# RWKV stage of a one-core decoder step: eight gate steps of each pair placed elsewhere, the h chunk loaded in halves, constants and states loaded after the first h

## The chip, the core and the metric

The program runs on one core of a Trainium2 chip. The metric is the device time of one execution in microseconds, lower is better. A number is the median of several executions; one further execution is profiled, and all rows below are from that one.

## What is computed

One layer of a hybrid decoder over 1024 prompt rows and 8 x 8 sample rows (1088 columns in the transposed layout that the kernel uses). Only the RWKV branch, and the sigmoid gates that the merge needs later, are touched by the change:

```python
mixed = cur + (prev - cur) * p['rwkv_mu']
r, wd, k, v, ad, gd = _split(mixed, RWKV_SPLIT)
w_log = -jax.nn.softplus(-(p['rwkv_w0'] + jnp.tanh(wd) @ p['rwkv_w2'])) - 0.5
decay = jnp.exp(-jnp.exp(w_log))
a = jax.nn.sigmoid(p['rwkv_a0'] + ad @ p['rwkv_a2'])
kk = kk / jnp.maximum(jnp.linalg.norm(kk, axis=-1, keepdims=True), 1e-12)
...
def step(state, inp):
    r_t, w_t, k_t, v_t, a_t, b_t = inp
    sa = jnp.einsum('bhvk,bhk->bhv', state, a_t)
    state = (state * w_t[:, :, None, :] + sa[..., None] * b_t[:, :, None, :]
             + v_t[..., None] * k_t[:, :, None, :])
    return state, jnp.einsum('bhvk,bhk->bhv', state, r_t)
...
merged = (jax.nn.sigmoid(gate_a) * (att @ p['w_branch_a'])
          + jax.nn.sigmoid(gate_b) * (rwkv_y @ p['w_branch_b']))
```

gate_a and gate_b are h @ w_in for 2 x 1024 columns, h being the normed input. They depend on nothing of the RWKV recurrence.

## The kernel before

The program is a row of stages, each a block in which the five engines run their own instruction streams and meet through semaphores: norm, projections and index scores, `rwkv`, attention, merge and MLP, final norm. Stages follow one another, so what `rwkv` gains or loses moves all behind it.

`rwkv` has two jobs. The first is the recurrence, in four rounds (pairs of heads, `for i in range(HP)`, called pair 0 to pair 3 here). A round has these parts. (1) `prelude`: VectorE (DVE) mixes rows and makes decay, normed keys and the scaled operands `ar`, `kt`, `bt`; ScalarE (ACT) does sigmoids, roots and exponentials; TensorE (PE) only does some sums over channels (L1162, L1168, L1174, L1180). It ends with three waits of PE, on `tilde` (operands made), `bon_done` (L1685) and `act_nrm`. (2) `products` (L1193), masked by DVE (L1692). (3) Five levels of a block inversion with 32 x 32 matmuls, `level_p` (L1207) and `level_x` (L1216, L1220), DVE keeping each result (L1699 to L1720), transposes `turn` (L1245) and `weigh_values` (L1258) between them, then `last_p`, `last_x` (L1228, L1236). ACT copies their results (`keep_last_p`, `assemble`, L1545 to L1555). (4) The inversion proper and the carries, `for g in range(4)`: `invert` (L1270), `ends` (L1284 and on), `carry` (L1313, L1318), where `keep_ends` and `keep_state` of DVE (L1733 to L1746) make each state that the next `carry` needs. (5) The sample rows, `sample(i, step)`, and (6) `normalise`.

The second job is filler: the 2048 gate columns, 16 blocks of 128 columns (gate columns from here on) for each of three chunks of h, `CH` = 384, 384 and 320 wide, so 48 gate columns of 8 accumulating matmuls. The generator `gate(count)` issues the next `count` of these 384 matmuls (gate steps) wherever it is called (L1154). A step leaves two records in the trace, as all f32 matmuls here. All gate columns share one PSUM bank, `B[:, GB]`: the first step of a gate column waits until ACT has read the one before (`gate_kept`, by `keep_gate`, L1491), and for its weights `w_gate` (two buffers, 512 KB each, loaded by ACT's queue, L1476). `keep_gate(n)` stands at a fixed place in ACT's stream, and ACT does nothing else until gate column n is made. h lies in `hc`, one buffer of 8 x 384 columns, loaded whole by `load_h` from inside `keep_gate(15)` and `keep_gate(31)`, and at the stage's start. The first step of gate columns 0, 16 and 32 waits for it.

A round holds 96 steps (88 in round 0): before the change 40 or 48 of them in the prelude, 24 in the levels, 8 in the inversion, 8 with the samples, 8 in `normalise`.

At the stage's start SP's queue loads, in this order, `low`, `w2a2`, three raw rows (`load_raw`), the constants `cst` (128 x 2624), `gd`, `g2` and the sample states; ACT's queue loads h and two `w_gate` at the same time.

## Time and profile before

| | |
|---|---|
| median of 3 runs | 2753.6 us (2742.47 to 2755.73) |
| profiled execution, its own time | 2749.19 us |
| its span, first to last instruction | 2747.4 us |
| mean granted TensorE clock | 0.941 of full speed |
| `rwkv`, from its first DMA issue to its last gate step | 535.3 to 1315.5 us |
| PE, DVE, ACT busy in the span | 89%, 51%, 27% |

How to read it: the profiled execution lies inside the range of the runs, and its own time is 1.8 us over its span. The busy shares are means over stages with different limits, so the rows that count are those of the `rwkv` stage alone.
### The profile page before, as it was taken

The numbers are of one execution on the slowest core, as the hardware profiler recorded it, in microseconds if no ns is written. First come the engines' busy times: TensorE is split into PE (matmuls) and PEld (weight loads), VectorE is DVE, ScalarE is ACT, GpSimd is POOL, SyncE is SP. The second block draws the span as 40 slices with busy tenths as digits, with TensorE's granted clock in tenths as the row PEclk, the third lists the DMA queues.
The fourth block names the chain that finished last, engine by engine and source line by source line (L and its number), as shares of the span: only waits on it lengthen the run. The fifth ranks groups of instructions, "written<-read, shape, count | busy, mean of one in ns | idle before, by whom it ended". The sixth has DMA issues, their size and how long they took to land. (4 is left out here: it accounts for less than half of the span.)

```text
span 2747.4 us, 52951 instructions
## 1 busy us (share of the span) xinstructions
PE 2453.7 (89%) x22029; PEld 1842.6 (67%) x22029; DVE 1414.5 (51%) x3009; ACT 729.8 (27%) x1370; POOL 92.8 (3%) x133
## 2 busy tenths in 40 slices
PE   7989999677887887878688988999999999999998
PEld 4566888545555555556466556778888888888886
DVE  3348888651552632723556665656533543543543
ACT  3226887022222212302345543112100100100101
POOL 0110000000100100100110110000000000000000
PEclk8989999898988888888899999999999999999999
DMA  6432223331321322311777774421111111111111
GB/s 173 119 94 80 88 71 96 111 94 35 87 84 35 87 62 67 86 34 36 233 246 231 251 253 163 133 71 31 47 41 37 47 41 36 47 42 36 47 31 73
DMA packets 289085, 252.45 MB, mean 92 GB/s; under 512 B 53528, under 2 KB 240506, under 8 KB 288719
## 3 DMA queue, kind: packets, MB, share of 16 engines
q1 hardware_dynamic: 211382, 198.89, 23.3%
q10 hardware_dynamic: 77464, 50.18, 6.6%
q8 instruction: 174, 2.85, 0.4%
q14 instruction: 65, 0.52, 0.1%
HBM read 200.43 MB, written 48.59 MB: 91 GB/s over the span
## 5 line engine op out<-in xcount | busy, mean ns | idle before, releaser
L1154 PE MATMUL rwkv_banks<-h_chunk,w_gate 128*128 128x384 f32 (+1 forms) x768 | 296.4, 531 | 32.9 <-ACT gate_rows L1491 13.3
L2615 DVE TENSOR_TENSOR x<-x,ps_mm 128x272 f32<-128x272 f32 x280 | 121.1, 436 | 307.8 <-PE ps_mm L2582 307.7
L2606 ACT COPY merged_then_hidden<-ps_mm 128x272 f32<-128x272 f32 x160 | 61.7, 386 | 720.6 <-PE ps_mm L2582 720.6
L1154 PEld LDWEIGHTS rwkv_banks<-h_chunk,w_gate 128*128 128x128 f32 x768 | 155.7, 214 | 129.8 <-issue 61.4
L2582 PE MATMUL ps_mm<-merged_then_hidden,w_mm 128*128 128x272 f32 x960 | 227.1, 393 | 1.6 <-DVE sums_of_right_sides_ L2835 0.9
L2582 PEld LDWEIGHTS ps_mm<-merged_then_hidden,w_mm 128*128 128x128 f32 x960 | 182.2, 190 | 39.9 <-DVE sums_of_right_sides_ L2835 1.3
L2582 PE MATMUL ps_mm<-v_T_and_gates_then_h_mlp,w_mm 128*128 128x272 f32 x864 | 204.5, 392 | 0.0
L2582 PEld LDWEIGHTS ps_mm<-v_T_and_gates_then_h_mlp,w_mm 128*128 128x128 f32 x864 | 164.1, 190 | 33.9
L2582 PE MATMUL ps_mm<-sums_of_right_sides_,w_sums_mm 128*128 128x272 f32 x704 | 165.3, 392 | 0.6 <-DVE sums_of_right_sides_ L2793 0.6
L2582 PEld LDWEIGHTS ps_mm<-sums_of_right_sides_,w_sums_mm 128*128 128x128 f32 x704 | 133.7, 190 | 28.5 <-issue 1.0
L2615 DVE TENSOR_TENSOR merged_then_hidden<-merged_then_hidden,ps_mm 128x272 f32<-128x272 f32 x120 | 51.6, 435 | 195.3 <-PE ps_mm L2582 195.2
L556 PE MATMUL first_banks<-hT,w_pr 128*128 128x384 f32 (+3 forms) x432 | 146.9, 498 | 4.2 <-PEq L188 4.2
L866 DVE TENSOR_SCALAR_CACHE_REDUCE idx_pages<-scores,mid 128x384 f32<-128x384 f32 (+4 forms) x150 | 131.5, 877 | 3.1
L2582 PE MATMUL ps_mm<-att_T,w_sums_mm 128*128 128x272 f32 x544 | 128.1, 392 | 0.0
L556 PEld LDWEIGHTS first_banks<-hT,w_pr 128*128 128x128 f32 (+1 forms) x432 | 82.2, 195 | 63.0 <-issue 22.8
L2582 PEld LDWEIGHTS ps_mm<-att_T,w_sums_mm 128*128 128x128 f32 x544 | 103.4, 190 | 21.3
L2152 PE MATMUL turned_or_scored_ps<-ident,k_pages 128*128 128x128 f32 x512 | 82.9, 287 | 10.4 <-DMA k_pages<-in_cache_k 7.5
L775 ACT ACTIVATE idx_pages<-idx_pages 128x1024 f32<-128x1024 f32 (+1 forms) x60 | 90.1, 1503 | 0.0
L675 PE MATMUL first_banks<-sums_of_right_sides,w_pr 128*128 128x274 f32 x320 | 80.6, 405 | 6.7 <-DVE gate_in L917 5.7
L2582 PE MATMUL ps_mm<-sums_of_right_sides_,w_mm 128*128 128x272 f32 x352 | 84.8, 393 | 1.4 <-DVE merged_then_hidden L2615 1.4
L2152 PEld LDWEIGHTS turned_or_scored_ps<-ident,k_pages 128*128 128x128 f32 x512 | 58.4, 145 | 35.6 <-issue 19.7
L1491 ACT ACTIVATE gate_rows<-rwkv_banks 128x384 f32<-128x384 f32 (+1 forms) x48 | 22.8, 475 | 216.4 <-PE rwkv_banks L1154 216.3
(475 smaller groups left out, 4296.3 us busy)
## 6 DMA issues: line engine op xcount, KB each, us to landing
k_pages<-in_cache_k SPq DMA_DIRECT2D x128, 256.0 KB, 3.4
v_pages<-in_cache_v SPq DMA_DIRECT2D x128, 256.0 KB, 5.2
w_gate<-in_w_in ACTq DMA_DIRECT2D x48, 512.0 KB, 4.1
w_mm<-in_w_mlp_in SPq DMA_DIRECT2D x32, 512.0 KB, 4.9
w_mm<-in_w_mlp_out SPq DMA_DIRECT2D x32, 512.0 KB, 4.6
w_pr<-in_w_in SPq DMA_DIRECT2D x27, 512.0 KB, 5.2
v_T_and_gates_then_h_mlp<-gates_T SPq DMA_DIRECT2D x16, 544.0 KB, 4.6
gates_T<-gate_rows ACTq DMA_DIRECT2D x32, 192.0 KB, 4.1
```

What stands on the lines that cost most here:

```text
L556: ins = MM(B[0:width, 6 + q % 2, 0:m], wk[:, k, 0:width], p.hT[:, k, t0:t0 + m], start=(k == 0), stop=(k == KO - 1))
L675: ins = MM(product(u, step, c), left[step][:, k, :], right[step][:, k, c * W2:c * W2 + W2], start=(k == 0 and step in ("P1", "P2", "P5")), ...
L775: nc.scalar.activation(scratch, scratch, ACT.Sign, accum_out=cnt[0:m, j:j + 1])\
L866: ch.done(V.tensor_scalar(above[0:m, 0:x.shape[1]], x, mid[0:m, j:j + 1], 0.0, ALU.is_gt, ALU.add, accum_out=cnt[0:m, j:j + 1]))
L1154: ins = MM(B[:, GB, 0:w], gw[:, n % 2, k, :], hc[:, k, 0:w], start=(k == 0), stop=(k == KO - 1))
L1491: nc.scalar.activation(gr[:, n % 2, 0:w], B[:, GB, 0:w], ACT.Sigmoid).then_inc(S["gate_kept"], 1)
L2152: ins = nc.tensor.transpose(to[:, g * 128:g * 128 + 128], kp[:, J % 3, g, c * 128:c * 128 + 128], p.ident[:, :])
L2582: ins = self.nc.tensor.matmul(self.ps[:, c, self.BANK[step], 0:272], left[step][:, k, :], right[step][:, k, 272 * c:272 * c + 272], start= ...
L2606: self.nc.scalar.copy(self.target(step, rows, c), self.out(act, u, step, c)).then_inc(self.by_act, 1)
L2615: self.nc.vector.tensor_tensor(to, to, ps, ALU.add).then_inc(self.by_dve, 1)
```

## The change

It does three things.

1. Eight gate steps leave the end of each prelude (`gate(16)` becomes `gate(8)`) and come back later in the round: two behind `last_x`, and two in each of g = 1, 2 and 3, between the two last carries. Two steps of level 3 are placed one half-level or one level later. ACT's `keep_gate` calls are placed to fit: three instead of four gate columns with the prelude of round 0, the next one now ahead of `keep_rows(3)` instead of behind it, and one behind `keep_y` for g = 1 and for g = 3.
2. `load_h` issues two DMAs, rows 0 to 3 and 4 to 7 of `hc`, each with a semaphore; step 0 waits for the first, step 4 for the second.
3. At the start SP waits until both halves of the first h have landed before it issues `cst`, `gd`, `g2` and the states.

```diff
             load_raw(0)
+            for half in range(2):
+                sp.wait_ge(h_in[half], 16)
             sp.dma_start(cst[:, :], const_d).then_inc(S["once_in"], 16)
...
-                        if n % (2 * KO) == 0:
-                            pe.wait_ge(S["h_in"], 16 * (n // (2 * KO)) + 16)
                         if n:
                             pe.wait_ge(S["gate_kept"], n)
+                    if n % (2 * KO) == 0 and k % (KO // 2) == 0:
+                        pe.wait_ge(h_in[k // (KO // 2)], 16 * (n // (2 * KO)) + 16)
...
-                gate(16)
+                gate(8)
...
-                    gate(3 if l < 4 else 2)
+                    gate((3, 3, 3, 1, 2)[l])
...
-                    gate(2)
+                    gate(2 if l < 3 else 3)
                 for L in range(2):
                     last_p(i, L)
                 for L in range(2):
                     last_x(i, L)
+                gate(2)
...
                         carry(i, 4 * g - 2)
+                        gate(2)
                         carry(i, 4 * g - 1)
...
-                act.dma_start(hc[:, :, 0:w], p.h_d[:, :, t0:t0 + w].rearrange("k p t -> p k t")).then_inc(S["h_in"], 16)
+                for half in range(2):
+                    ks = slice(half * KO // 2, (half + 1) * KO // 2)
+                    act.dma_start(hc[:, ks, 0:w], p.h_d[ks, :, t0:t0 + w].rearrange("k p t -> p k t"))\
+                        .then_inc(h_in[half], 16)
...
-                for n in range(2, 5):
+                for n in range(2, 4):
...
-                keep_gate(12 * i + 5)
+                    if t == 2:
+                        keep_gate(12 * i + 4)
...
-                for n in range(6, 8):
+                for n in range(5, 7):
...
-                    if g == 3:
-                        keep_gate(12 * i + 8)
                     keep_y(i, g)
+                    if g in (1, 3):
+                        keep_gate(12 * i + 7 + g // 2)
```

PE's stream in round 0, from the last inversion matmuls (L1228, L1236) to the first of `ends`, before (L1154 is the gate, L1270 `invert`, L1245 `turn`):

```order
L1154 MATMUL rwkv_banks<-h_chunk,w_gate 128x384 x2
L1228 MATMUL rwkv_banks<-X_XT_by_quads,AA 32x32 x32
L1236 MATMUL rwkv_banks<-X_XT_by_quads,masked_product 32x32 x32
L1270 MATMUL rwkv_banks<-AV_and_a_rows,XT_of_chunks 64x128 x8
L1245 MATMUL rwkv_banks<-ident,prev_minus_k 128x128
```

and now (all lines of PE's code are three further down, so L1157 is the gate and L1273 `invert`):

```order
L1157 MATMUL rwkv_banks<-h_chunk,w_gate 128x384 x3
L1231 MATMUL rwkv_banks<-X_XT_by_quads,AA 32x32 x32
L1239 MATMUL rwkv_banks<-X_XT_by_quads,masked_product 32x32 x32
L1157 MATMUL rwkv_banks<-h_chunk,w_gate 128x384 x2
L1273 MATMUL rwkv_banks<-AV_and_a_rows,XT_of_chunks 64x128 x8
L1248 MATMUL rwkv_banks<-ident,prev_minus_k 128x128
```

The last gate group ahead of `last_p` has three steps instead of two, and two steps stand between `last_x` and `invert`, where none stood.

PE's stream in round 0 between two carries of g = 1, before:

```order
L1313 MATMUL rwkv_banks<-state_before_chunk,carry_of_chunk 64x64 x2
L1318 MATMUL rwkv_banks<-r_with_carry,state_before_chunk 64x64 x2
L1313 MATMUL rwkv_banks<-state_before_chunk,carry_of_chunk 64x64 x2
L1318 MATMUL rwkv_banks<-r_with_carry,state_before_chunk 64x64 x2
L1245 MATMUL rwkv_banks<-ident,prev_minus_k 128x128
```

and now:

```order
L1316 MATMUL rwkv_banks<-state_before_chunk,carry_of_chunk 64x64 x2
L1321 MATMUL rwkv_banks<-r_with_carry,state_before_chunk 64x64 x2
L1157 MATMUL rwkv_banks<-h_chunk,w_gate 128x384 x2
L1316 MATMUL rwkv_banks<-state_before_chunk,carry_of_chunk 64x64 x2
L1321 MATMUL rwkv_banks<-r_with_carry,state_before_chunk 64x64 x2
L1248 MATMUL rwkv_banks<-ident,prev_minus_k 128x128
```

Two steps stand between the carries; nothing else differs there. The same holds for g = 2 and 3.

ACT's stream in round 0, around the third and fourth `keep_rows` (L1530, L1534), before:

```order
L1530 COPY k_b_v_rows<-rwkv_banks 128x384
L1534 COPY AV_and_a_rows<-rwkv_banks 128x2x64
L1530 COPY k_b_v_rows<-rwkv_banks 128x384
L1534 COPY AV_and_a_rows<-rwkv_banks 128x2x64
L1491 ACTIVATE gate_rows<-rwkv_banks 128x384
```

and now (L1538 and L1542 are the two copies, L1499 the sigmoid of a gate column, L1481 and L1503 its DMAs):

```order
L1538 COPY k_b_v_rows<-rwkv_banks 128x384
L1542 COPY AV_and_a_rows<-rwkv_banks 128x2x64
L1499 ACTIVATE gate_rows<-rwkv_banks 128x384
L1481 DMA w_gate<-in_w_in 128x8x128
L1503 DMA gates_T<-gate_rows 128x384
L1538 COPY k_b_v_rows<-rwkv_banks 128x384
L1542 COPY AV_and_a_rows<-rwkv_banks 128x2x64
```

The sigmoid that stood behind both copies now stands between them.

## Rows read from the trace of the kernel before

**Rows 1.** Who waited for whom: PE over 535 to 1320 us; total us, times, longest.
```profile
PE rwkv_banks L1313 <- DVE state_before_chunk L1746: 18.0, 20, 1.3
PE rwkv_banks L1220 <- issue: 17.9, 11, 2.7
PE rwkv_banks L1216 <- issue: 17.8, 9, 3.2
...
PE rwkv_banks L1154 <- ACT gate_rows L1491: 13.3, 17, 1.2
...
PE rwkv_banks L1270 <- ACT XT_of_chunks L1555: 5.8, 4, 1.5
```

**Rows 2.** Timeline, DVE and PE, end of pair 0's prelude: start, us, what.
```profile
588.44 1.41 DVE L1685 TENSOR_TENSOR bonus<-rwkv_banks,raw_v 128x384 f32<-128x384 f32 x3
...
590.08 5.40 PE L1154 MATMUL rwkv_banks<-h_chunk,w_gate 128*128 128x384 f32 x16 [0.67 <-ACT gate_rows L1491]
595.41 0.46 PE L1193 MATMUL rwkv_banks<-a_r_tilde,prev_minus_r 64*64 64x128 f32 x8
```

**Rows 3.** Timeline, DVE and PE, end of pair 1's prelude.
```profile
778.86 1.41 DVE L1685 TENSOR_TENSOR bonus<-rwkv_banks,raw_v 128x384 f32<-128x384 f32 x3
...
783.65 6.94 PE L1154 MATMUL rwkv_banks<-h_chunk,w_gate 128*128 128x384 f32 x16 [6.39 <-DMA h_chunk<-h_T]
790.52 0.46 PE L1193 MATMUL rwkv_banks<-a_r_tilde,prev_minus_r 64*64 64x128 f32 x8
```

**Rows 4.** Timeline, DVE and PE, ends of the preludes of pairs 2 and 3.
```profile
973.46 1.41 DVE L1685 TENSOR_TENSOR bonus<-rwkv_banks,raw_v 128x384 f32<-128x384 f32 x3
...
977.87 0.46 PE L1193 MATMUL rwkv_banks<-a_r_tilde,prev_minus_r 64*64 64x128 f32 x8
...
1166.22 1.41 DVE L1685 TENSOR_TENSOR bonus<-rwkv_banks,raw_v 128x384 f32<-128x384 f32 x3
...
1162.59 4.54 PE L1154 MATMUL rwkv_banks<-h_chunk,w_gate 128*128 128x320 f32 x16 [0.62 <-ACT gate_rows L1491]
1167.74 0.47 PE L1193 MATMUL rwkv_banks<-a_r_tilde,prev_minus_r 64*64 64x128 f32 x8 [0.60 <-issue]
```

**Rows 5.** Timeline of PE, pair 0: inversion and first carries.
```profile
663.68 1.97 PE L1270 MATMUL rwkv_banks<-AV_and_a_rows,XT_of_chunks 64*64 64x128 f32 x16 [1.46 <-ACT XT_of_chunks L1555]
...
666.49 1.86 PE L1154 MATMUL rwkv_banks<-h_chunk,w_gate 128*128 128x384 f32 x4
...
680.44 0.33 PE L1313 MATMUL rwkv_banks<-state_before_chunk,carry_of_chunk 64*64 64x64 f32 x4 [1.32 <-DVE state_before_chunk L1746]
...
684.65 1.56 PE L1154 MATMUL rwkv_banks<-h_chunk,w_gate 128*128 128x384 f32 x4
```

**Rows 6.** Busy us (x instructions) by stretch of pair 0: PE PEld DVE ACT POOL, clock, DMA, GB/s.
```profile
656.00:668.00 12.00, 10.49 (x156) 7.55 (x154) 0.86 (x3) 7.20 (x18) 0.00 (x0) 0.53 0.23 61
668.00:698.00 30.00, 23.22 (x576) 18.73 (x576) 7.44 (x23) 7.03 (x18) 0.00 (x0) 1.00 0.10 27
698.00:712.00 14.00, 12.19 (x99) 8.28 (x96) 4.88 (x15) 1.06 (x2) 0.00 (x0) 0.63 0.34 122
```

**Rows 7.** DMA issues over 535 to 560 us: KB each, median us to landing.
```profile
w_gate<-in_w_in ACTq DMA_DIRECT2D x2, 512.0 KB, 22.5
...
raw_v<-proj_T SPq DMA_DIRECT2D x1, 548.0 KB, 10.9
...
g<-in_rwkv_g SPq DMA_DIRECT2D x1, 256.0 KB, 15.8
```

**Rows 8.** DMA issues over 600 to 1320 us.
```profile
w_gate<-in_w_in ACTq DMA_DIRECT2D x41, 512.0 KB, 4.0
```

**Rows 9.** Timeline, PE and DVE: first gate column, first scan, wait for the norms.
```profile
557.84 7.21 PE L1154 MATMUL rwkv_banks<-h_chunk,w_gate 128*128 128x384 f32 x16 [9.14 <-DMA w_gate<-in_w_in]
...
557.16 2.42 DVE L1653 TENSOR_TENSOR_SCAN cum<-rwkv_const,log_decay 128x1088 f32<-128x1088 f32 x1
...
571.77 0.73 DVE L1672 TENSOR_SCALAR kk_norm<-kk_norm 128x1088 f32<-128x1088 f32 x1 [5.45 <-ACT kk_norm L1515]
```

More of the change, by code:

```diff
@@ L1060, in rwkv @@
         "s_yk": 1, "s_ya": 1, "s_sk": 1, "s_ot": 1, "s_ok": 2}
-    S = {n: p.sem("rw_" + n) for n in (*ROUND, "once_in", "lora_in", "pool", "dve", "h_in", "gate_made",
+    S = {n: p.sem("rw_" + n) for n in (*ROUND, "once_in", "lora_in", "pool", "dve", "gate_made",
                                        "gate_kept")}
@@ L1064, in rwkv @@
     gate_out = [p.sem(f"rw_gate_out{b}") for b in range(2)]
+    h_in = [p.sem(f"rw_h_in{half}") for half in range(2)]
     HS = [slice(64 * h, 64 * h + 64) for h in range(2)]
```

## Prediction, written before the changed kernel ran

> **What bounds the kernel now.** The stages run one behind the other, so I asked only whether a microsecond saved inside `rwkv` ends the stage earlier, and read the waits of PE over the stage, then the timeline at the places that the change touches. PE is never free for long there, but it is not the one bound. In the preludes DVE is a closed chain, and PE fills the time with gate steps. From `products` on PE sets the pace, held up by DVE's state, by ACT's copies and by "issue". [rows 1] shows the sizes: 18.0 us for 20 waits for DVE's state, 13.3 us for ACT reading the gate bank, 5.8 us for ACT's assembly ahead of `invert`, and 35.7 us (17.9 + 17.8) in 20 idle stretches inside `level_x` that end with "issue". The reader is to see that a gate step placed where PE is full costs its whole length and that one placed in a wait costs only what the wait doesn't hold.
>
> **Term 1, the end of the prelude.** `products` needs DVE's last prelude operation (L1685). In pair 0 that ends at 588.44 + 1.41 = 589.85, but PE starts `products` at 595.41, behind a block of eight steps that takes 5.40 us and began with 0.67 us of waiting [rows 2]. In pair 3 the order is reversed: PE starts 0.10 us after DVE's end (1166.22 + 1.41 = 1167.63, 1167.74) [rows 4], so 0.1 is what lies between the two when DVE is last. Without the block, PE starts there in every pair. Pair 0: 595.41 - 589.95 = 5.5. Pair 1: the block also waited 6.39 us for h and ran in 6.94, so 790.52 - (778.86 + 1.41 + 0.1) = 10.2 [rows 3]. Pair 2: 977.87 - 974.97 = 2.9. Pair 3: 0 [rows 4]. Sum 18.6 us. The second h is now needed only behind `products` and the first `level_p`, about 7 us later than DVE's end, and its load starts where it did (gate column 15 is made at the same time), so the 6.39 us are gone whole. This sum is bare reading and I take it as sure within 1 us.
>
> **Term 2, the first microseconds.** The first gate column starts at 557.84, the moment its weights land, after 9.14 us of waiting [rows 9]. These two `w_gate` took 22.5 us from issue to landing [rows 7], where 41 later ones took 4.0 [rows 8]. The whole start hangs on it: DVE waits 5.45 us for the norms that come through ACT and PE behind this gate column [rows 9]. After the change the constants (1.3 MB), `gd`, `g2` and the states aren't in flight until h has landed. When h landed no row shows; it is ahead of `w_gate` on its queue, so at the latest 4.0 us before 557.84, at the earliest near 547, when the raw rows land. I take 549. Then the weights have the engines nearly alone for a microsecond or two, and I expect the first gate column at about 554, 3.5 us earlier. Bounds: 0 if the constants catch up with the weights before they land, 5.45 because then DVE is the later one. The constants themselves: behind `raw_v` (landed 10.9 us after its issue) the three loads ended with `g2` (15.8 after its) took 4.9 us plus the spacing of their issues, some 7 in all; from 549 plus 1 to 2 us of start they land at about 558, and the scan that needs them began at 557.16 [rows 7, 9]. DVE is late by 1 us and has the 5.45 to hide it in. Term 2: 3.5 (0 to 5.5).
>
> **Term 3, ACT's place for the gate bank.** Of the 13.3 us of [rows 1], 17 waits, four are of 1.2 (one a pair: `gate(2)` of level 1 starts a new gate column while ACT is still held by `keep_rows(3)`, the order that the change turns round). The other 13 are about 0.65 each; one a pair lies inside `gate(3)` of level 3, where a gate column ended in mid-call. Both go: 4 x (1.2 + 0.65) = 7.4. Against it stand the stretches that end with "issue". They come inside `level_x`, where PE runs hundreds of tiny matmuls, and if they depend on how many instructions went by in how much time, a wait removed just ahead of one makes it longer by the same amount. I take 6.5, bounds 0 and 7.4.
>
> The Trainium skill, "Runtime: NRT & Kernel Launch", section "Instruction fetch mechanics", says that instructions are fetched in blocks of 256 while the last block is executed and that this is mostly hidden. By it the 7.4 would be kept whole. This trace doesn't bear the "hidden" out: 35.7 us of PE's idle time in this stage end with "issue", up to 3.2 at a time [rows 1].
>
> **Term 4, what the moved steps cost.** Two behind `last_x`: the wait there is 1.46 us, 5.8 over the pairs [rows 1, 5]. Two steps take 1.56 us when the clock is up and 1.86 in the neighbouring group [rows 5]; this stretch runs at 0.53 [rows 6], at which they would take 3.1. So 0.1, 0.4 or 1.6 us a pair; I take 0.5, sum 2 (0 to 6.5). Three times two between carries: each wait is 1.32 us (12 of the 20 waits of the first row in [rows 1]), and the steps take 1.56 [rows 5] at a clock of 1.00 [rows 6], less for the 320-wide chunk: 12 x 0.24 = 2.9 at most, I take 2. While they run DVE makes the state, so nothing else is late. Behind the new `keep_gate` of g = 1 ACT has `keep_rows(7)`, for which `weigh_values(3)` waits; the sigmoid and two DMA issues take more than the carry and the transpose that PE does meanwhile. An uncovered turn of ACT costs PE 0.67 [rows 2]; I take 0.25 a pair, 1 in all (0 to 3). In pair 2 the third h is loaded from this place, and its first half is needed in g = 2, where in pair 0 4.2 us pass between the carry and the next gate group (680.44 to 684.65) [rows 5]; the same call now issues two loads ahead of its sigmoid. I take 0.5 (0 to 3).
>
> **Term 5, the clock at the start of the levels.** PE now stands still at the prelude's end: in pair 3 the block of 4.54 us with its 0.62, and the 0.60 behind it, become 5.8 us of idling [rows 4], in pairs 1 and 2 about 3, in pair 0 less than 1. After 6.39 us without work a block of eight steps took 6.94 instead of 5.40 us [rows 3], 1.5 more. I take this price for pairs 1 to 3: 4.5 (0 to 9, as `products` and `level_p` may do too little work to bring it back).
>
> **Sum.** Gains 18.6 + 3.5 + 6.5 = 28.6; costs 2 + 2 + 1 + 0.5 + 4.5 = 10. Net 18.6, so the profiled execution, 2749.2 by its own time, would take 2730.6, and the median, 2753.6, would become 2735. The profiled one lies 4.4 us under that median and the runs spread over 13 us, which is as much as the effect; I say 2736. About 0.5% (13.8 us) is what a measurement of this kernel can tell from no change.
>
> **Rivals.** (a) As forecast, net gain 14 to 24: 0.48. (b) The gain at the prelude is there but is given back: the "issue" stretches take all of term 3, term 5 costs 9, term 4 its upper bounds for two of its parts. Then 22 - 9 - 8 = 5, or 2748. For it speaks that these stretches stand in every pair; against it that term 1 alone is 18.6 and read off directly. With all mixtures that stay under 13.8: 0.35. (c) More than forecast: the start gives 5.5, term 5 nothing since the gate group of level 0 follows at once, and the filled waits keep the clock up in the sample part, which now stands at 0.63 for 14 us [rows 6]. At full speed its busy 12.2 us would shrink by up to a third; 2 us a pair give 8. Net 30, or 2724: 0.11. (d) Slower: the clock. If the eight moved steps all run at 1.2 GHz, they cost 8 x 0.68 = 5.4 us more a pair, 21.6 in all, which leaves -3; and if `products` to the first carries stay at that speed too, a stretch of PE work such as the 23.2 us in 668 to 698 [rows 6] becomes nearly twice as long. It decides from about 4 us a pair beyond the first 21.6, and at 10 us a pair the time would be 2796. Nothing in the rows shows so long a cold stretch behind a wait of 3 us: 0.06.
>
> The Trainium skill, "TensorE: Matmul & The Clock Gate", part 1, says that the default state is throttled and that activity releases it, so waiting for DVE at full idleness is the worse way to spend the same time. The row at 783.65 agrees, with 6.94 against 5.40 us.
>
> **Range and chances.** The likeliest case gives 2730 to 2740 about 2736. The range takes in (c) and nearly all of (b): 2722 to 2752. Faster by over 0.5%: (a) almost whole and (c), 0.57. Within 0.5%: (b) and the edge of (a), 0.37. Slower: 0.06.
>
> **What would show it.** Right: in pairs 0 to 2 `products` starts about 0.1 us after L1685 (now L1688), as in pair 3; no wait for h anywhere of over 1 us; the waits of 1.32 between carries and of 1.46 ahead of `invert` gone; no ACT wait of 1.2 at the gate; `w_gate` at the start landing in under 20 us; the scan at 557 to 559. Wrong: "issue" idle time of much over 36 us in the stage; a granted clock of 0.5 through the levels; PE waiting for h in g = 2 of pair 2; DVE's scan later than 562.

## The result, and the profile after

| | runs | median | profiled execution | its span | clock |
|---|---|---|---|---|---|
| before, its three earlier runs and three beside after | 6 | 2742.22 us (2739.55 to 2755.73) | 2749.19 us | 2747.4 us | 0.941 |
| after | 6 | 2722.16 us (2714.29 to 2726.8) | 2714.29 us | 2712.5 us | 0.946 |

The ratio is 0.9908, 95% interval 0.9886 to 0.9929: 0.9% faster, some 20 us by the medians. The two profiled executions lie 34.9 us apart, because the one of before is slower than its median and the one of after is the fastest of six. So the two profiles can't be subtracted as wholes; the first thing to read is which of their differences repeat.

The waits of PE over the stage of after (lines of PE's code are three further down than before; columns as in [rows 1]: total us, times, longest):

```profile
PE rwkv_banks L1223 <- issue: 22.8, 9, 4.2
PE rwkv_banks L1219 <- issue: 21.1, 10, 3.8
...
PE rwkv_banks L1196 <- issue: 15.3, 3, 5.8
...
PE rwkv_banks L1261 <- ACT AV_and_a_rows L1542: 8.0, 8, 2.5
...
PE rwkv_banks L1157 <- ACT gate_rows L1499: 3.9, 6, 0.7
...
PE rwkv_banks L1210 <- issue: 2.6, 6, 0.6
PE rwkv_banks L1196 <- DVE bonus L1694: 2.5, 1, 2.5
PE rwkv_banks L1157 <- DMA w_gate<-in_w_in: 2.3, 1, 2.3
PE rwkv_banks L1316 <- DVE state_before_chunk L1755: 2.1, 8, 0.3
PE rwkv_banks L1248 <- issue: 2.0, 1, 2.0
PE rwkv_banks L1157 <- issue: 1.2, 1, 1.2
...
PE rwkv_banks L1273 <- ACT XT_of_chunks L1563: 0.8, 2, 0.4
```

Against [rows 1]: the state waits went from 18.0 to 2.1 us, ACT at the gate bank from 13.3 to 3.9, the assembly from 5.8 to 0.8, and no row waits for h. New is L1196, `products`: PE now stands idle ahead of it in every pair, 2.5 us in pair 0 and 15.3 in the other three. The profile writes "issue" for those three, but PE starts `products` 0.1 us after DVE's last prelude operation there, so they are waits for DVE. The two `level_x` rows that end with "issue" grew from 35.7 to 43.9; with the other lines of the levels (6.3, 4.1 and 2.4 us before; 2.6, 2.0 and 1.2 here, L1210, L1248 and L1157) it is 48.5 and 49.7.

The end of pair 0's prelude, timeline of DVE and PE, answers to [rows 2]:

```profile
578.83 1.41 DVE L1694 TENSOR_TENSOR bonus<-rwkv_banks,raw_v 128x384 f32<-128x384 f32 x3
...
580.50 0.47 PE L1196 MATMUL rwkv_banks<-a_r_tilde,prev_minus_r 64*64 64x128 f32 x8 [2.48 <-DVE bonus L1694]
```

DVE ends at 580.24 and PE starts 0.26 later; in pairs 1 to 3 it is 0.10. The block of eight steps that stood between them is gone.

The DMA issues at the stage's start (answers to [rows 7]), then PE's first gate column and DVE's scan (answers to [rows 9]):

```profile
w_gate<-in_w_in ACTq DMA_DIRECT2D x3, 512.0 KB, 13.9
rwkv_const<-rwkv_constants SPq DMA_DIRECT2D x1, 1312.0 KB, 6.0
...
g<-in_rwkv_g SPq DMA_DIRECT2D x1, 256.0 KB, 8.3
```

```profile
546.53 1.84 PE L1157 MATMUL rwkv_banks<-h_chunk,w_gate 128*128 128x384 f32 x3 [2.25 <-DMA w_gate<-in_w_in]
...
554.43 2.42 DVE L1662 TENSOR_TENSOR_SCAN cum<-rwkv_const,log_decay 128x1088 f32<-128x1088 f32 x1 [1.78 <-DMA g<-in_rwkv_g]
```

The weights land 13.9 instead of 22.5 us after their issue (each the median of the issues in the window). The stage itself begins at 531.55 in this profile and at 535.34 in that of before, with the same instructions ahead of it, so times are best counted from there: the first gate column starts at 15.0 instead of 22.5, the scan at 22.9 instead of 21.8.

For all kernels below I divided the stage at four kinds of marks in the trace and subtracted. "Products 0" is the start of pair 0's products, counted from the stage's first DMA issue. A prelude runs from the first L1165 to the first L1196 of its pair. Levels run from the first product to the first matmul of `last_x`, inversion from there to the first transpose of the samples (L1330), samples from there to the next prelude. The last three are sums over four pairs. All in us, one profiled execution each:

```
kernel             products 0  preludes 1, 2, 3   levels  inversion  samples  stage  time (median, ratio to before)
before                 60.1    56.1  48.8  46.4    266.9    149.7     152.2   780.1  2742.2
after                  48.9    45.9  45.9  46.3    256.1    148.9     158.4   750.5  2722.2  0.9908
e9  after again        49.0    45.9  45.9  46.3    259.1    150.7     156.9   753.9  2722.8  0.9935
e1  start only         52.6    55.2  48.8  47.1    255.6    153.2     152.3   764.9  2730.9  0.9955
e2  steps only         54.6    45.9  45.9  46.4    264.0    149.0     155.2   761.0  2727.8  0.9938
e3  no wait of SP      54.5    45.9  45.9  46.4    265.5    146.9     156.2   761.3  2724.3  0.9922
e12 first half only    54.4    45.9  45.9  46.3    267.6    147.8     152.3   760.2  2726.4  0.9942
e7  ACT late           49.2    45.9  45.9  46.3    262.6    151.7     155.9   757.7  2720.6  0.9936
e5  all in levels      48.9    45.9  45.9  46.3    273.7    156.3     157.8   774.9  2737.5  0.9998
e6  six in prelude     49.7    54.0  45.9  46.4    246.9    155.1     156.0   754.0  2719.0  0.9934
e4  spread             49.2    45.9  45.9  46.4    253.6    148.2     154.3   743.6  2704.1  0.9855
e10 spread again       48.6    45.9  45.9  46.3    251.4    149.0     157.1   744.2  2707.8  0.9871
e8  even               49.2    46.6  46.6  46.9    258.5    144.3     150.8   742.9  2711.4  0.9908
e11 even, 4 in prelude 49.8    46.6  46.6  46.9    253.6    144.6     151.2   739.2  2707.0  0.9874
```

The reader is to see two kinds of columns. The first four repeat within 0.6 us where the kernels are alike there, and can be read off one profile. The levels do not: five kernels with the very same levels (after, e9, e2, e3, e12; "the five" below) give 256.1 to 267.6, 262.5 in the mean. The median of before, measured beside each group of kernels, was 2744.2 (e1 to e4, 11 runs), 2738.75 (e5 to e8, 17 runs) and 2741.67 us (e9 to e12, 16 runs); a difference between two kernels of different groups is best taken by their ratios to it. The ratio is taken within a group and has an interval of 0.15 to 0.25%, 4 to 7 us, either way.

The granted clock over the levels differs as well. It is 0.83 to 0.86 in before, the five, e7 and e6, 0.91 in e1, 0.89 in e5, and 0.89, 0.93, 0.92 and 0.92 in e4, e10, e8 and e11.

### The profile page after: what moved, and what is told of

Its sections match the earlier page's. It is cut to its first block and busy times, and to the rows that moved or that the text cites. A ratio compares the mean times of both kernels' runs of the same rounds, so it can differ in the third digit from the quotient of the medians.

```text
span 2712.5 us, 52956 instructions
## 1 busy us (share of the span) xinstructions
PE 2442.5 (90%) x22029; PEld 1838.0 (68%) x22029; DVE 1413.5 (52%) x3009; ACT 729.3 (27%) x1370; POOL 92.7 (3%) x133
## 5 line engine op out<-in xcount | busy, mean ns | idle before, releaser
L1157 PE MATMUL rwkv_banks<-h_chunk,w_gate 128*128 128x384 f32 (+1 forms) x768 | 293.0, 525 | 7.4 <-ACT gate_rows L1499 3.9
L1157 PEld LDWEIGHTS rwkv_banks<-h_chunk,w_gate 128*128 128x128 f32 x768 | 152.5, 210 | 93.3 <-issue 31.2
L2591 PEld LDWEIGHTS ps_mm<-sums_of_right_sides_,w_mm 128*128 128x128 f32 x352 | 66.7, 190 | 15.7 <-DVE merged_then_hidden L2624 2.1
```

Source lines behind the costliest of these rows:

```text
L1157: ins = MM(B[:, GB, 0:w], gw[:, n % 2, k, :], hc[:, k, 0:w], start=(k == 0), stop=(k == KO - 1))
L2591: ins = self.nc.tensor.matmul(self.ps[:, c, self.BANK[step], 0:272], left[step][:, k, :], right[step][:, k, 272 * c:272 * c + 272], start= ...
```

## The experiments

**e1, the start alone.** The kernel before with parts 2 and 3 of the change (halves of h, SP's wait), and `gate(16)` and all else as it was.

> The kernel before with the halves of h and the constants behind h, and no gate step moved. Theory: the start is a gain of its own, since both DVE and PE hang on the first gate column; DVE's last prelude operation of pair 0 should stand 5 to 6 us earlier after the stage's first DMA issue than the 54.5 us before, and PE's products too, still 5 us behind it, because the block of eight steps stands there. The halves may take 0 to 3 us from the 6.4 us that pair 1 waits for h. Time 5 to 9 us under before (ratio 0.997 to 0.998). Rival: the start only uncovers DVE's wait for the constants, so products move less than 2 us and the ratio is 0.999 to 1.000.

Measured: 2730.88 us, ratio 0.9955 (0.9938 to 0.9972). DVE's last operation stands at 48.5 us, 6.0 earlier, as the theory had it. Products of pair 0 start 7.4 us earlier (60.1 to 52.6), pair 1's prelude is 0.9 shorter and pair 3's 0.7 longer. So the readable part is 7.6 us, inside the theory's 5 to 9, but the median came out 13 us lower, outside it. The levels of this profile are 11 us under those of before with the same instructions, and their clock is 0.92, 0.92, 0.89 and 0.90 by pair where before has 0.90, 0.84, 0.85 and 0.83. One profile can't tell whether that is chance, so why the median fell by 13 and not by 8 stays open.

**e2, the steps alone.** The kernel before with part 1 of the change only.

> The kernel before with the gate steps and ACT's calls moved, h whole and the constants where they were. Theory: the prelude gain of 18.6 us stands alone (5.5, 10.2, 2.9 and 0 us in pairs 0 to 3), and what follows costs nothing net, so the time is 17 to 22 us under before (ratio 0.992 to 0.994), and products start 0.1 to 0.3 us behind DVE's last operation in all pairs. Rival (the one on record): the moved steps cost what they take in the inversion part and in the cold clock, about 10 us in sum, so the ratio is 0.996 to 0.998.

Measured: 2727.77 us, ratio 0.9938 (0.9923 to 0.9954), 16 us under before. The marks moved by 5.5, 10.2, 2.9 and 0.0 us, exactly the forecast's reading of them. Levels, inversion and samples together take 568.2 us against 568.8 before: the moved steps cost nothing that this pair of profiles shows. The ratio lies inside the first theory's 0.992 to 0.994; the 16 us are just under its 17 to 22.

**e3, SP's wait taken out of after.**

```diff
             load_raw(0)
-            for half in range(2):
-                sp.wait_ge(h_in[half], 16)
```

> The kernel after with the one wait of SP taken out: the constants, gd, g2 and states are issued at once again, h stays in halves. Theory: the wait is what brings the first weights early, so they land at about 22 us after their issue again instead of 14, and the time is 4 to 6 us over after (ratio to before about 0.993). Rival: the halves alone give most of it, because the first half of h lands early and its packets are smaller; then the time is within 2 us of after.

Measured: 2724.29 us, ratio 0.9922 (0.9904 to 0.9941). The weights land 20.9 us after their issue and products of pair 0 start at 54.5, as in e2 (54.6), where h is whole. So all 5.6 us of the start (54.5 to 48.9) come from the wait and none from the halves. The medians lie only 2.1 us apart, and intervals of this width can't tell 0 from 5.6; by the times the rival would stand as well, and the marks decide against it.

**e12, SP waits for the first half only.** The same two lines replaced by `sp.wait_ge(h_in[0], 16)`.

> The kernel after with SP waiting for the first half of h only. DVE is now the later engine at the start (its scan waits 1.8 us for the constants, PE idles 2.5 us ahead of the products of pair 0). Theory: the constants are issued 5 us earlier and land 1.5 to 3 us earlier, the scan starts 1 to 1.8 us earlier, the first weights land at most 2 us later, so products of pair 0 start at 47.2 to 48.2 us instead of 49 from the stage's first DMA issue; the time is within 2 us of after. Rival: the constants then run beside the second half of h and the weights, which land 3 us or more later, and products start at 50 us or later.

Measured: 2726.42 us, ratio 0.9942 (0.9924 to 0.9959). The rival holds: products start at 54.4. The issues at the start of this kernel, and its first gate column, which stands 22.5 us after the stage's first issue:

```profile
w_gate<-in_w_in ACTq DMA_DIRECT2D x3, 512.0 KB, 21.2
rwkv_const<-rwkv_constants SPq DMA_DIRECT2D x1, 1312.0 KB, 9.9
...
g<-in_rwkv_g SPq DMA_DIRECT2D x1, 256.0 KB, 12.3
```

```profile
554.02 6.24 PE L1156 MATMUL rwkv_banks<-h_chunk,w_gate 128*128 128x384 f32 x14 [8.15 <-DMA w_gate<-in_w_in]
```

Here the constants are issued at 7.6 us, when the first half of h lands, instead of at 13.6, and that cost all that was won: the first gate column starts 7.5 us later and products 5.5. Of the three moments tried (at once, behind the first half, behind both) only the last lets the weights run ahead of the constants. The Trainium skill, "DMA: Bandwidth & Descriptors", section "Queues, rings and completion order", says that an engine takes turns between queues and switches only at packet boundaries. That would explain why short rows of weights (512 B) lose against the constants' rows of 10.5 KB (2624 f32) on the other queue. The trace has packets of these two sizes and the landing times agree; no run here changed the packets, and in e12 more bytes are in flight as well, so the cause itself is not shown.

**e5, all steps in the levels.** After with its eight moved steps put into the levels, 32 instead of 24 there, and ACT's calls placed to fit.

```diff
-                    gate((3, 3, 3, 1, 2)[l])
+                    gate((4, 4, 4, 1, 2)[l])
...
-                    gate(2 if l < 3 else 3)
+                    gate((4, 4, 3, 3, 3)[l])
...
-                gate(2)
                 for g in range(4):
...
                         carry(i, 4 * g - 2)
-                        gate(2)
```

> The kernel after with the eight moved steps put into the levels' gate groups instead of behind last_x and between the carries (32 steps there instead of 24, in groups of 3 or 4). Theory A (the levels are held to the pace at which PE's instructions arrive, so steps there are nearly free): the levels grow by 0 to 2 us a pair, the idle time that ends with issue shrinks by 3 to 5 us a pair, the waits for DVE's state and for the assembly come back (4.6 and 0.8 us a pair) where steps of 5.5 us stood; the time is within 5 us of after. Theory B (those stretches have a fixed length): the levels grow by 5.5 us a pair, the idle time stays, and the time is 17 to 22 us over after, 2739 to 2744.

Measured: 2737.52 us, ratio 0.9998 (0.9981 to 1.0015). That is 15 us over after by the medians, 17 (against e9) or 25 us by the ratios, theory B's 17 to 22 within the noise. Its waits:

```profile
PE rwkv_banks L1223 <- issue: 22.4, 12, 3.8
PE rwkv_banks L1219 <- issue: 21.4, 14, 4.4
PE rwkv_banks L1316 <- DVE state_before_chunk L1753: 17.8, 20, 1.3
...
PE rwkv_banks L1273 <- ACT XT_of_chunks L1561: 6.9, 4, 1.9
```

The waits of [rows 1] are back (17.8 and 6.9) and the inversion is 156.3 us long with 8 fewer steps a pair in it; the levels grew by 11 us against the mean of the five, 2.8 a pair. Neither theory has that right: A said 0 to 2, B 5.5; and the idle time that ends with "issue" didn't shrink by A's 3 to 5 a pair (45.9 us with all lines, 49.7 in after). What is settled is the place: between the carries and behind `last_x` eight steps a pair don't lengthen the inversion, and in the levels they cost.

**e6, six steps in the prelude's wait.** After with `gate(14)` instead of `gate(8)` at the prelude's end, and `gate((2, 2, 2, 0, 2)[l])` and `gate(2)` in the levels, ACT's calls placed to fit.

> The kernel after with six steps of each pair's levels put behind the last prelude block, where PE now stands idle for 2.5 us in pair 0 and 4.8 to 5.8 in the others (14 steps there, 18 in the levels). Theory B: the levels shorten by 4.1 us a pair and pair 0's products come 1.6 us later, so the time is 13 to 15 us under after. Theory A: the levels shorten by under 1.5 us a pair, the idle time that ends with issue grows by 3 to 4 us a pair, and the time is 0 to 5 us under after. In both the clock at the start of products shows what the idling cost: 6.3 us for the products before, under 5.3 if the clock is kept up.

Measured: 2718.95 us, ratio 0.9934 (0.9913 to 0.9956). The levels took 246.9 us, the lowest of all, 15.6 under the mean of the five. Some 5 of that are the products (below), and the rest is 0.4 us for each of the 24 steps, between A's price and B's; e5 gives 0.35 (11.2 us for 32). Pair 1 lost 8 us of it, since its extra steps begin the second h chunk and wait 4.6 us for it, and the inversion is 6 us longer than in the five; the time is A's, level with e9 (0.9935). The products of pair 2, timeline of PE, first of after and then of e6:

```profile
937.83 2.74 PE L1157 MATMUL rwkv_banks<-h_chunk,w_gate 128*128 128x384 f32 x8
945.36 0.72 PE L1196 MATMUL rwkv_banks<-a_r_tilde,prev_minus_r 64*64 64x128 f32 x8 [4.78 <-issue]
...
948.36 0.74 PE L1196 MATMUL rwkv_banks<-a_r_tilde,prev_minus_k 64*64 64x128 f32 x8
```

```profile
957.35 0.47 PE L1196 MATMUL rwkv_banks<-a_r_tilde,prev_minus_r 64*64 64x128 f32 x8
...
962.18 0.75 PE L1210 MATMUL rwkv_banks<-rwkv_const,AA 32*32 32x32 f32 x64
```

Eight products take 0.74 us after an idle stretch of 4.78 and 0.47 without one; all of them take 6.29 us (945.36 to 951.65) in after and 4.90 (957.35 to 962.25) in e6. The granted clock over these stretches, of after and then of e6 (the stretch, its length, busy us of PE, PEld, DVE, ACT, POOL; then clock, DMA share, GB/s), is 0.66 and 1.00:

```profile
945.30:952.00 6.70, 6.54 (x176) 6.07 (x179) 4.11 (x7) 0.00 (x0) 0.00 (x0) 0.66 0.02 6
```

```profile
957.30:963.00 5.70, 5.05 (x193) 4.28 (x192) 4.38 (x8) 0.00 (x0) 0.00 (x0) 1.00 0.02 4
```

**e7, ACT late.** After with ACT's fifth gate column behind `keep_rows(3)` again and the levels' groups of before, `gate(3 if l < 4 else 2)` and `gate(2)`.

> The kernel after with ACT's fifth gate column behind keep_rows(3) again and the levels' groups of the kernel before (3, 2 in each; level 4 has 2, 2); the eight moved steps stay where they are. Theory B: PE waits for ACT 1.9 us more in each pair and the time is 6 to 8 us over after. Theory A: these waits come back in the trace, but the idle time that ends with issue shrinks by as much, and the time is within 3 us of after.

Measured: 2720.61 us, ratio 0.9936 (0.9914 to 0.9958), level with the 0.9935 of e9. Its waits:

```profile
PE rwkv_banks L1223 <- issue: 18.4, 10, 2.4
...
PE rwkv_banks L1219 <- issue: 14.6, 7, 2.7
...
PE rwkv_banks L1157 <- ACT gate_rows L1499: 11.4, 14, 1.2
...
PE rwkv_banks L1210 <- issue: 4.0, 7, 1.1
...
PE rwkv_banks L1157 <- issue: 2.5, 1, 2.5
...
PE rwkv_banks L1248 <- issue: 2.1, 1, 2.1
```

ACT's waits are back, 11.4 against 3.9 us, and what ends with "issue" in the levels fell from 49.7 (22.8 + 21.1 + 2.6 + 2.0 + 1.2) to 41.6 (18.4 + 14.6 + 4.0 + 2.5 + 2.1) us. The sums, 53.0 and 53.6, are the same. This is theory A: ACT's order, with the gate groups that go with it, brought nothing that these runs show; the interval leaves room for a few us either way.

**e4 and e10, spread.** After with the same 24 steps a pair, one or two of each level between the two calls of `level_x`:

```diff
-                    gate((3, 3, 3, 1, 2)[l])
-                    for L in range(2):
-                        level_x(i, L, l)
+                    gate((2, 2, 2, 1, 1)[l])
+                    level_x(i, 0, l)
+                    gate((1, 1, 1, 1, 2)[l])
+                    level_x(i, 1, l)
...
-                    gate(2 if l < 3 else 3)
+                    gate(2)
```

> The kernel after with the same 24 gate steps in the levels, but one or two of each level put between the two calls of level_x instead of ahead of both. Nothing else is moved and no gate column ends elsewhere than between the same two copies of ACT. Theory A: the idle time that ends with issue is what is left when PE asks for instructions faster than they come, so steps put among the tiny matmuls fill it; that idle time falls from 49.9 us in the levels of all pairs by 5 to 15 us, and the time by the same. Theory B: these stretches are of fixed length whatever stands around them; idle time and time stay within 3 us of after.

> The spread kernel again, beside after. Theory A: it is faster than after every time, by 8 to 18 us (ratio to before 0.984 to 0.988), with the idle time that ends with issue in the levels again near 41 us. Rival: the first result was a lucky phase of the clock (0.953 against 0.944), and it lands within 5 us of after.

Measured: 2704.12 us (four runs), ratio 0.9855 (0.9836 to 0.9875), and again, beside e9, 2707.8 us, ratio 0.9871 (0.9847 to 0.9896). That is 15 to 18 us under after both times. The levels take 253.6 and 251.4 us, 9 to 11 under the mean of the five. The longest rows that end with "issue", of e4 and then of e10:

```profile
PE rwkv_banks L1223 <- issue: 15.5, 14, 2.1
PE rwkv_banks L1219 <- issue: 14.3, 11, 3.0
```

```profile
PE rwkv_banks L1219 <- issue: 16.1, 14, 3.0
PE rwkv_banks L1223 <- issue: 16.0, 14, 2.4
```

They fell from 43.9 to 29.8 and 32.1 us, in more and shorter stretches. With all lines it is 41.1 and 46.8 us against 49.7, so the second run misses the expected 41, and the idle time explains 3 to 9 us of the gain; the rest is not accounted for by any wait.

A second thing changed with the order and repeats: the granted clock. Over the whole program it is 0.949 to 0.956 in the ten executions of the spread kernel, and 0.942 to 0.946 in the twelve of after. Over the levels of pairs 0 to 3 it is 0.92, 0.84, 0.92, 0.88 in e4 and 0.97, 0.91, 0.94, 0.90 in e10, against 0.89, 0.86, 0.86, 0.83 in after. So the rival "a lucky phase of the clock" is out as chance, but the clock may carry a part of the gain as an effect of the order. No run here holds one of the two and moves the other.

**e8 and e11, even.** The spread kernel with 28 steps in the levels (3, 7, 6, 6, 6 by level), one step each less ahead of `ends` in g = 1 and 2 and in both groups of `normalise`, with ACT's `keep_gate` calls moved to fit. e11 puts four of the 28 behind the last prelude block, except in pair 1: `gate(8 if i == 1 else 12)`.

> Built on the spread kernel: the levels' steps by the number of instructions of a level (3 in level 0, 6 or 7 in each of the others, one group ahead of, one between, one behind the two calls of level_x; 28 instead of 24), taken from where PE is the bound and nothing waits: two of the steps ahead of ends, two of normalise. Theory A: the levels take no longer than in the spread kernel, the idle time that ends with issue falls by 2 to 3 us a pair, what follows the levels is 2.8 us a pair shorter; the time is 5 to 11 us under the spread kernel (2704), so 2693 to 2699. Theory B: the levels grow by 2.7 us a pair, what follows shrinks by that, and the time stays at 2702 to 2706.

> The even kernel with four of its 28 level steps put behind the last prelude block, in all pairs but pair 1 (whose next column would wait for h). Theory: products start at the same time as before in pairs 2 and 3 and run at the full clock there (4.9 us instead of 6.3 to 6.45), the levels are 0.5 us shorter for each step that left them, 2 us a pair; in sum 6 to 9 us under the even kernel, so 2702 to 2706 by its 2711, and about the time of the spread kernel or 3 us less. Rival: the idle time that ends with issue takes the place of the steps, as it took the place of ACT's waits; then only the 2.8 us of the products are gained.

Measured: e8 2711.41 us, ratio 0.9908 (0.9886 to 0.9931); e11 2707.01 us, ratio 0.9874 (0.9851 to 0.9897). e8 missed: inversion and samples are 7 us shorter than in e4, but the levels 5 us longer and each prelude 0.6 longer, and the ratio is 0.9908 against 0.9855 and 0.9871 of the spread kernel, slower than either theory had it. e11's products take 4.9 us as in e6 and its stage is the shortest, 739.2 us; its time is 4.4 us under that of e8, between its theory's 6 to 9 and its rival's 2.8, and that of the spread kernel.

**e9, after again.**

> The kernel after, unchanged, profiled and timed a second time, to see which differences between two profiles are the same every time. The preludes should repeat within 0.5 us (45.9, 45.9 and 46.4 us in pairs 1 to 3; products of pair 0 at 49 us from the stage's first DMA issue). The levels of all pairs, 256.1 us in the first profile of after and 264.0 and 265.5 in two kernels with the same levels, are expected anywhere in 255 to 266, and the time at 2716 to 2726. If instead the levels come out at 256 again, the layouts do differ and the reading that the moved steps cost nothing is wrong by up to 8 us.

Measured: 2722.75 us, ratio 0.9935 (0.9912 to 0.9958). The first four columns repeat within 0.1 us, the levels come out at 259.1, inside the expected 255 to 266. The time is that of the first measurement.

## Why the prediction was right or wrong

Forecast: 18.6 us faster, 2736. Measured: 2722.16 and 2722.75, which is 20.1 and 18.9 us under the medians of before taken beside them. The difference was right and the level was not. **The step that failed** is the starting point of the sum, "the median, 2753.6, would become 2735": that median was the middle one of three runs, two of which were high. With the three runs beside after it is 2742.22, and beside the later kernels 2738.8 to 2744.2. It accounts for 11 of the 14 us between 2736 and 2722.16. That the time is nevertheless inside the range (its lower end is 2722), and close to rival (c)'s 2724, is luck: (c)'s net gain of 30 did not come.

Behind the level the sum came out for partly wrong reasons. **The term that failed** is term 3, taken at 6.5 and worth 0. Term 4's cost of 5.5, which also came out at about 0, and 2 us more in term 2 made up for it, so that the net of 18.6 is in part luck:

**Term 1** (18.6) was exact, part by part: 5.5, 10.2, 2.9, 0 (e2).

**Term 2** (3.5, bounds 0 to 5.5): 5.6, a little over the upper bound. The landing of h was read well, 549 or 13.7 us after the stage's first issue against 13.5 measured. The weights were put 5 us behind it, at 18.7, and landed 1.4 behind it, at 14.9. With that DVE became the later engine, as the upper bound had it. Its wait of 5.45 us for the norms is gone whole, and so is the next one, which the forecast didn't count. Of before:

```profile
582.18 1.29 DVE L1676 SCALAR_TENSOR_TENSOR a_r_tilde<-kk,cum_before 128x1088 f32<-128x1088 f32 x1 [1.37 <-ACT cum L1522]
```

Against these 6.8 us stands the scan, 1.1 later because it waits 1.8 us for `g2`; the difference, 5.8, is what DVE's last operation moved (54.5 to 48.7).

**Term 3** (6.5, bounds 0 and 7.4): 0. The waits went as read (13.3 to 3.9), but the idle time that ends with "issue" took their place, the lower bound that I had named and passed over. e7 shows it by putting the waits back. I leaned on their size; the row beside them, nearly three times as large, was the one that decided. What the record adds on how it took their place stands in the last section.

**Term 4** (5.5, two kinds of steps and two waits): 0 or a gain. The inversion is 146.9 to 150.7 us long with sixteen steps a pair in it (the five), 151.7 and 155.1 in e7 and e6, and 149.7, 153.2 and 156.3 with eight (before, e1, e5). The working priced each step at its length less the wait that it fills (and two steps at the 0.53 of [rows 6] at 3.1 us, where 1.56 / 0.53 gives 2.9; nothing hangs on it). It left out that the clock rises with the filled waits: over the inversions of the single pairs it is 0.87 to 0.91 in the three kernels with eight steps (before, e1, e5) and 0.91 to 1.00 in the five. In pair 1 it was 0.91 and is 1.00 now, and the stretch is 1 us shorter with 3.8 us more of busy PE in it. First before, then after:

```profile
855.10:892.80 37.70, 29.48 (x664) 23.83 (x664) 7.44 (x23) 12.95 (x33) 0.00 (x0) 0.91 0.14 37
```

```profile
826.40:863.10 36.70, 33.24 (x681) 24.68 (x681) 7.46 (x24) 13.26 (x34) 0.00 (x0) 1.00 0.15 40
```

Within one code the clock has its price too: pair 2's inversion takes 38.1 us at 1.00 in after and 40.0 at 0.91 in e9. In pair 2 one wait of 2.5 us for ACT came up (L1261, 8.0 against 5.9 us in all, the feared place of the two loads in `keep_gate(31)`), within the bounds given.

**Term 5** (4.5, bounds 0 to 9): the mechanism and the size held at its place. The products take 5.75, 6.29, 6.29 and 6.45 us instead of 4.90, together 5.2 us. The idle stretches ahead of them were read too short, at under 1, about 3, about 3 and 5.8 us; they are 2.5, 4.8, 4.8 and 5.8. The length alone doesn't set the price: in e10 pair 0's products take 4.89 us behind 3.8 us of idling. The term was also incomplete: the samples of pairs 2 and 3 also run colder, at 0.70 and 0.74 instead of 0.73 and 0.83, and all samples take 155 to 158 us instead of 152 in four of the five profiles.

Terms 3 to 5 as a whole: levels, inversion and samples take 563.4 to 568.6 us in the five kernels with the new arrangement (mean 566.9), 568.8 and 561.1 with the old (before, e1; mean 565.0). So +2, with a scatter of 4 either way, where the forecast had +3.5. Taken from the 24.2 us gained at the marks (5.6 + 18.6) it leaves 22 us, between the 19 to 20 of the medians and the 25 of the first ratio.

By its difference the forecast itself, (a) with a net gain of 14 to 24, is what came. Of the rivals (b), the gain given back, did not come: "issue" took term 3, but term 4 cost nothing. (c) was right on the start and the inversion's clock and wrong on the samples. (d) did not come: over all levels the clock is 0.86 in after and 0.85 in before. Of the signs, `products` behind L1694, the waits for h, state, assembly and ACT, the landing of `w_gate` and the scan (558.2 on the clock of before's profile) came as written. The one that said "wrong", issue time of much over 36 us, did light up (43.9) and was half right: term 3 was lost to it, but over all lines of the levels it had not grown (48.5 and 49.7).

## What to carry to other kernels

Cut both traces at marks and subtract part by part, and profile one kernel twice, before believing a difference: here the parts that hang on one wait repeated within 0.6 us and the levels scattered by 11 us with the same instructions, so that one pair of profiles "showed" 35 us where the medians have 20. Take the starting point of a forecast from more than three runs when they spread as far as the effect. A wait removed just ahead of a stretch limited by something else (here the arrival of instructions) may be worth nothing: name that limit first. In these runs filler in a real wait cost nothing, and the clock was up with it; and filler put in among streams of tiny matmuls was worth more than the same filler ahead of them.

## What the runs showed of the hardware

**Idle time at fixed instruction counts.** The stretches that end with "issue" in the levels lie whole multiples of 256 instructions apart. Busy us and, in brackets, instructions of PE and PEld in after, cut at five such stretches of pair 0 (each window ends in one):

```profile
604.60:616.40 11.80, 9.76 (x383) 6.83 (x383) 2.23 (x4) 1.02 (x3) 0.00 (x0) 0.86 0.02 4
616.40:619.88 3.48, 2.89 (x128) 1.93 (x128) 0.69 (x1) 0.00 (x0) 0.00 (x0) 1.00 0.02 5
619.88:623.70 3.82, 2.75 (x127) 2.00 (x128) 0.85 (x2) 0.86 (x2) 0.00 (x0) 1.00 0.11 17
623.70:628.80 5.10, 1.30 (x128) 1.20 (x128) 0.69 (x1) 0.00 (x0) 0.00 (x0) 0.68 0.48 135
628.80:640.15 11.35, 9.30 (x384) 6.57 (x383) 2.78 (x6) 0.00 (x0) 0.00 (x0) 0.84 0.02 4
```

That is 766, 256, 255, 256 and 767 instructions, or 3, 1, 1, 1 and 3 times 256 but for a record or two; the stretches of the other pairs lie likewise. None of the five took under 3.48 us for 256; the fourth, with 1.30 us of work in it, took 5.10. The Trainium skill, "Runtime: NRT & Kernel Launch", section "Instruction fetch mechanics", gives this block of 256 instructions, and the count agrees. It says that crossing a block is mostly hidden, and the rows say that for blocks of tiny matmuls it is not: 49.7 us in this stage.

The loads of instructions themselves are in the traces, and they settle what these stretches wait for. DMA queue q8 moves 174 packets of 16 KB in every one of the kernels, one for each 253 of PE's 44058 matmuls and weight loads. Two of them in after, in windows 617.5 to 618.6 and 626.4 to 627.5 (packets, MB, share of 16 engines):

```profile
q8 instruction: 1, 0.02, 5.4%
...
q8 instruction: 1, 0.02, 5.5%
```

The first lands at 618.55 and PE goes on at 619.93, the second at 627.46 and PE goes on at 628.87. In all fourteen traces the levels hold 369 stretches of over 0.5 us that end with "issue", and every one ends 1.0 to 1.6 us after such a load has landed (median 1.4). The two closest loads of each trace's levels start 3.2 to 3.4 us apart. So blocks with less work than that in them are paced by the loads.

**A weight load in front of an instruction load.** The second load above starts 5.5 us after the one before it, where that one had come 3.4 behind the first. Ahead of it ran a load of `w_gate`, issued here and landed 4.1 us later, just before the instruction load starts at 626.50:

```profile
622.26 0.37 ACTq L1481 DMA_DIRECT2D w_gate<-in_w_in  x1
```

The stretch behind it is 3.8 us long. This too holds in all traces: each of the 42 stretches of over 3.1 us waits for an instruction load that starts 2.5 to 4.5 us after the issue of a `w_gate` load. Counting all stretches whose instruction load starts 2.5 to 5.3 us after such an issue, they hold 10.6 us in before, 25.4 and 25.2 in after and e9, 10.8 in e7, 14.4 and 17.1 in e4 and e10; all others hold 35.7, 23.7 and 22.7, 30.6, 24.5 and 27.0. So with the new order of ACT, which also places these loads, more and longer stretches of this kind came up, and the spread kernels' smaller idle time lies in this kind alone. No run moved a weight load by itself, so what that would bring is not shown. How much of the spread kernel's 15 to 18 us comes from the idle time and how much from the clock stays open.

**Idling and the clock.** 4.78 us of idle PE ahead of the products of pair 2 cost 1.39 us in the next 6 (granted clock 0.66 over them, a mean of its two levels of 1.2 and 2.4 GHz), and 4.80 us in pair 1 as much.

**A load that starts early can cost more than it brings.** Constants issued behind the first half of h instead of the second delayed the first gate column by 7.5 us (15.0 to 22.5).
